# A split-precision projection stream on Trainium2: GpSimd's low halves of two k-tiles in one instruction

## The reference

```python
def hybrid_layer(x, norm_g, w_in, w_out, ...):
    h = rms_norm(x, norm_g)
    p = jnp.einsum('btd,dp->btp', h, w_in)          # (512, 2048) x (2048, 7192)
    (aq, ak, av, alr, az, bq, bk, bv, bz, cq, ck, cv, cz, dqkv, dbeta, da, dz) = jnp.split(p, offs, axis=-1)
    ya = gla_mixer(aq, ak, av, alr, ...) * jax.nn.silu(az)
    yb = swa_mixer(bq, bk, bv, ...) * jax.nn.silu(bz)
    yc = diff_mixer(cq, ck, cv, ...) * jax.nn.silu(cz)
    yd = gdn_mixer(dqkv, dbeta, da, ...) * jax.nn.silu(dz)
    y = jnp.concatenate([ya, yb, yc, yd], axis=-1)
    return x + jnp.einsum('btm,md->btd', y, w_out)  # (512, 2048) x (2048, 2048)
```

## Time and profile before

| | us |
|---|---|
| median of 3 runs | 1945.56 |
| lowest, highest | 1944.40, 1947.06 |
| the profiled execution | 1945.65 |
| its span, first to last instruction | 1943.7 |
| TensorE busy (matmuls) | 1919.0 |
| GpSimd busy | 919.0 |
| of it the low halves, 576 instructions | 753.5 |
| of it the issue of 288 fetches | 163.7 |

### The profile page before, as it was taken

One profiled execution on the slowest core, in us unless ns is written; L12 is line 12 of the kernel. 1 busy time (PEld: TensorE's weight loads), 2 busy tenths in 40 slices (PEclk: granted clock), 3 DMA queues, 4 the chain that ended last, 5 costly groups with the idle time before them and its releaser, 6 DMA issues.

```text
span 1943.7 us, 25935 instructions
## 1 busy us (share of the span) xinstructions
PE 1919.0 (99%) x10824; PEld 1554.6 (80%) x10824; DVE 682.7 (35%) x1234; ACT 495.5 (25%) x998; POOL 919.0 (47%) x876
## 2 busy tenths in 40 slices
PE   6999999999999999999999999999999999999999
PEld 5888788778888888777888887788788888887787
DVE  2656233223111343543324561332231113435442
ACT  4110222022222343322221011222132224433230
POOL 3555443444555543444554554434445554444454
PEclk9999999999999999999999999999999999999999
DMA  8566454545555556555775665444455555564556
GB/s 277 158 192 194 132 148 133 149 134 152 172 166 171 163 152 217 152 152 168 220 224 151 194 174 152 140 136 137 141 162 167 168 167 172 152 228 139 153 172 197
DMA packets 92180, 326.94 MB, mean 168 GB/s; under 512 B 10174, under 2 KB 10912, under 8 KB 91040
## 3 DMA queue, kind: packets, MB, share of 16 engines
q0 software_dynamic: 41472, 151.01, 27.4%
q1 hardware_dynamic: 44288, 155.75, 26.4%
q10 hardware_dynamic: 6304, 18.52, 2.5%
HBM read 316.86 MB, written 8.39 MB: 167 GB/s over the span
## 4 chain that ended last, share of the span: by engine, by line
PE 96%; ACT 2%; DMA 1%; DVE 1%; issue 0%; SPq 0%
PE acc L492 81%; PE mix L769 1%; PE mix L788 1%; DMA slots<-in_x 1%; PE mix L582 1%; PE mix L569 1%; PE mix L861 1%; PE mix L573 1%; PE mix L831 1%; PE mix L747 1%; PE mix L816 1%; PE mix L717 1%; PE mix L599 1%; PE mix L552 1%; PE mix L544 1%; PE mix L779 0%
## 5 line engine op out<-in xcount | busy, mean ns | idle before, releaser
L453 POOL TENSOR_TENSOR w_lo<-w_raw,w_hi 128x512 fp32r<-128x512 f32 x576 | 753.5, 1308 | 692.7 <-DMA w_hi<-in_wstream 525.9
L492 PE MATMUL acc<-w_hi,actT_hi 128*128 128x512 f32 x1920 | 781.7, 407 | 2.9 <-ACT slots L943 2.9
L492 PE MATMUL acc<-w_hi,actT_lo 128*128 128x512 f32 x1920 | 750.8, 391 | 0.0
L492 PE MATMUL acc<-w_lo,actT_hi 128*128 128x512 f32 x1920 | 749.4, 390 | 0.0
L492 PEld LDWEIGHTS acc<-w_hi,actT_hi 128*128 128x128 f32 x1920 | 361.0, 188 | 92.1 <-issue 22.1
L492 PEld LDWEIGHTS acc<-w_hi,actT_lo 128*128 128x128 f32 x1920 | 360.4, 188 | 78.3
L492 PEld LDWEIGHTS acc<-w_lo,actT_hi 128*128 128x128 f32 x1920 | 361.6, 188 | 65.0
L435 POOL DMA_DIRECT2D w_hi<-in_wstream x288 | 163.7, 568 | 322.6 <-PE acc L492 317.7
L492 PE MATMUL acc<-actT_hi,w_hi 128*128 128x512 f32 x384 | 152.1, 396 | 0.0
L492 PE MATMUL acc<-actT_hi,w_lo 128*128 128x512 f32 x384 | 149.8, 390 | 0.0
L492 PE MATMUL acc<-actT_lo,w_hi 128*128 128x512 f32 x384 | 149.6, 390 | 0.0
(11 more groups left out here) (247 smaller groups left out, 1699.6 us busy)
## 6 DMA issues: line engine op xcount, KB each, us to landing
w_hi<-in_wstream POOLq DMA_DIRECT2D x288, 512.0 KB, 3.9
w_raw<-in_wstream SPq DMA_DIRECT2D x288, 512.0 KB, 4.5
out_x<-slots ACTq DMA_DIRECT2D x7, 1024.0 KB, 8.2
slots<-in_x SPq DMA_DIRECT2D x4, 1024.0 KB, 15.5
slots<-in_x ACTq DMA_DIRECT2D x1, 4096.0 KB, 15.2
slots<-out_x ACTq DMA_DIRECT2D x1, 4096.0 KB, 15.7
out_x<-slots ACTq DMA_DIRECT2D x4, 256.0 KB, 2.2
cf_sb<-in_cf ACTq DMA_DIRECT2D x1, 933.0 KB, 11.3
```

The source lines that it names most:

```text
L453: pool.tensor_tensor(w_lo[:, n % RING], w_raw[:, g % RAW, k], w_hi[:, g % HI, k].bitcast(F32), ALU.subtract).then_inc(w_ready, 1)
L492: last = nc.tensor.matmul(acc[b][:, :], lhsT, rhs, start=(k == 0 and i == 0), stop=(k == kts - 1 and i == 2))
```

## The change

The two instructions of a pair become one over 1024 columns. It waits for the value of `kt_done` that the second of the two waited for (2g + 2), adds two to `w_ready`, and the fetch of w_hi for pair g + 1 is issued behind it. Nothing else differs: buffers, the other queues and the arithmetic are the same. The two k-tiles' buffers of `w_lo` lie next to each other (0 and 1, or 2 and 3).

```diff
                     pool.wait_ge(raw_in[g % RAW], g // RAW * 16 + 16)
                     pool.wait_ge(hi_in[g % HI], g // HI * 16 + 16)
-                    for k in range(2):
-                        n = 2 * g + k
-
-                        pool.wait_ge(kt_done, n + 1)
-                        pool.tensor_tensor(w_lo[:, n % RING], w_raw[:, g % RAW, k], w_hi[:, g % HI, k].bitcast(F32),
-                                           ALU.subtract).then_inc(w_ready, 1)
-                        if k == 0 and g + 1 < DEPTH * PAIRS:
-                            high_halves(g + 1)
+                    pe_done = 2 * g + 2
+                    pool.wait_ge(kt_done, pe_done)
+                    pool.tensor_tensor(w_lo[:, 2 * g % RING:2 * g % RING + 2], w_raw[:, g % RAW],
+                                       w_hi[:, g % HI].bitcast(F32), ALU.subtract).then_inc(w_ready, 2)
+                    if g + 1 < DEPTH * PAIRS:
+                        high_halves(g + 1)
```

## The result

The changed kernel takes 2271.65 us in the median of 4 runs (2263.41 to 2274.64), the kernel before 1944.98 us. The ratio is 1.167, with an interval of 1.164 to 1.170: slower by 327 us. The forecast was 2122 us with a range up to 2240, so the direction and the loop that sets the time held; the price of one member of that loop, the landing of w_hi's fetch, did not.

What follows compares the result with a forecast made beforehand. TensorE's matmuls bound the kernel, GpSimd's weight loop just ahead; lengthened to 7.07 us a pair, it costs 81 us in layer 0, 90 in layer 1 and 5 at the start: 176 us on 1945.65, so 2122 us, range 2030 to 2240.

Steps and rivals of the forecast that it cites:

- GpSimd's loop of operation, issue and landing: Weight supply on GpSimd: 5.47 us a pair before, 7.07 after; pairs with less TensorE work than that wait.
- The long operation: GpSimd's low halves: one 1024-column operation takes 2.40 us, between 2.29 and 2.59, replacing two of 1.295 us.
- The move as the cause: GpSimd's queue: the w_hi fetch, issued behind a 1.29 us operation before, now stands behind 2.40 us, lengthening each turn.
- Both fetches released within 0.1 us: GpSimd's w_hi and SyncE's raw fetch: one operation's end releases both; before, the raw issue came 1.92 us later.
- the landing of 4.5 us: w_hi's fetch, issue to landing, overlapping the raw fetch: 4.5 us likeliest, ends 3.9 and 5.1, against 3.9 before.
- the prediction's own table: Stretches of pairs with TensorE's time per pair; those under the loop's 7.07 us lose the difference: 81 and 90 us by layer.
- the 5 us of the start: First turns of the kernel: fetches take 5.3 to 7.0 us there, so 5 us were added to the sum.
- a sign of an error: TensorE's waits in the 7.48 us stretches, landings at 3.9 or over 5, or granted clock under 1.00 would show it wrong.
- the one of full hindrance: Rival on the two weight fetches: they hinder each other fully, loop 7.6 to 7.86 us, 2227 to 2300 us; chance 0.10.
- Cheap overlap: Rival on the two weight fetches: little hindrance, short operation, loop 6.39 to 6.6 us, 2005 to 2032 us; chance 0.09.
- not slower: Rival on w_hi's fetch: it gets quicker or its issue doesn't wait, time 1946 us; chance 0.03, of which 0.01 faster.
- The clock: Rival on TensorE: pauses every pair drop its clock to 1.2 GHz, some 700 us more, 2830 us; chance 0.02.

Runs made afterwards that it cites:

- the fetch first: Changed kernel with the next w_hi fetch issued ahead of the 1024-column operation instead of behind it: 1954.45 us, ratio 1.005.
- the move alone: Kernel before, two 512-column operations kept, with the next w_hi fetch issued behind the second instead of the first: 2294.10 us, ratio 1.178.
- the head start: Changed kernel with a small memset behind each w_hi issue; the raw fetch waits for it, issued 0.8 us after w_hi's: 2045.49 us, ratio 1.051.

## Why the prediction was wrong in its size

- *TensorE sets the end, GpSimd's loop of operation, issue and landing has no slack beside the short pairs.* Right. The chain that ended last consists of that loop now, and the landing and the operation as measured, pair by pair, followed through the loop and TensorE's own work of before, give 2253 us for the last k-tile's end, measured 2258.
- *The long operation, 2.40 us.* Right: 2384 ns in the mean, 2373 in the median.
- *The move as the cause, not the long operation.* Right: with the fetch first the loss is 10 us, with the move alone 349.
- *Both fetches released within 0.1 us.* Right, 0.08 us.
- **The step that failed: the landing of 4.5 us, with an end of 5.1.** It measured 5.0 in the median and 5.2 in the mean of the 280 fetches after the start. The working added 1.2 us ahead of the first byte, 2.65 us for both fetches at 395 GB/s, the rate of many queues at once, and 0.6 us behind the last byte: 4.45. The middle term is the one that was mis-sized; the two others came out shorter. In the changed kernel the first raw packet starts 1.04 us after w_hi's issue, from there to w_hi's last packet it is 3.59 us, and 0.37 us later the fetch lands. The two don't fill the engines together, they go one behind the other, at about 290 GB/s over both, with 236 GB/s while the raw fetch moves alone. Who goes first decides the rest: had it been w_hi's, its landing would be near 4.0, as with the head start. The raw fetch, issued 0.08 us later, gets its first packet out at 1.04 us, where w_hi's, undisturbed, needs 1.28. That quarter of a microsecond puts the raw fetch ahead. No row of before showed it: there the raw fetch starts beside w_hi's, 0.93 us after the end of its issue in place of 0.64. And the mean belongs in the sum, not the middle: each late fetch is lost for good in a loop without slack. Followed pair by pair, a landing of 5.0 throughout would end the last k-tile at about 2201 us, the mean of 5.19 at 2253.
- *Smaller misses.* The hop from landing to operation is 0.23 us now, where I had 0.11. And the landing of 5.1, with the operation at its likeliest 2.40, makes a loop of 7.67 us and by the prediction's own table 2251 us, over the end of the range at 2240. The rivals' times at 6.6, 7.6 and 7.86 us leave out the 5 us of the start, and the 0.7 us from the last bytes to the next operation are 0.93 by the rows that they were read from.
- *The price per stretch.* With 2.38 - 0.05 + 5.2 + 0.23 = 7.76 us in place of 7.07, the prediction's own table gives 158 + 168 us. Measured are 318. Layer 0 by stretch, forecast and measured: the start 11 and 11.7; the 19 short pairs 29.2 and 37.0; the 32 of 7.48 us 0 and 9.7; the 32 of 6.23 us 26.9 and 50.4; the 8 of 6.76 us 2.5 and 7.1; the 14 of 7.45 us 0 and 11.4; the 18 of 6.60 us 8.5 and 15.7; the last 8 pairs 7.7 and 17.8. The largest single miss, 23.5 us, is the 32 pairs of 6.23 us. Waits in the stretches of 7.48 us were named as a sign of an error, and they came.
- *The rival that came true* is the one of full hindrance, at 0.10: its loop of 7.6 to 7.86 us and 2227 to 2300 us hold the measured 7.8 and 2272. What was said for it, that a transfer can stand behind another one, is what happened; what was said against it, 2.65 us of work for both, is the term that failed.
- *Cheap overlap and not slower* fell with the 5.0 us. *The clock* did fall, in part, and cost next to nothing; see below.

## What to carry to other kernels

Where one engine's operation, the issue of the next fetch and that fetch's landing form a loop, add its members up before moving one behind another: the share of busy time (47% here) hides it. Look also at what else the same semaphore releases: the two transfers that start at one moment here don't share by halves, and 0.8 us of head start for the one that is waited for was worth 225 us. If two operations are merged, keep the issue ahead of them; that made the difference between 10 us and 327 us.

## What the hardware showed that I had not expected

A fetch issued by GpSimd, 128 rows of 4 KB, has its first packet 1.28 us after the issue, one issued by SyncE 0.64 us after the end of its own (0.97 after the start). When both are issued within 0.1 us, 128 rows of 4 KB each, SyncE's is served first and GpSimd's starts at 2.7 us. 64 rows of 4 KB beside it are worse than 128 rows (landing 5.5 against 5.0 us), which I can't explain.

The granted clock. It stayed full in the earlier trace rows; in the changed kernel it falls to half in 28 short stretches between 28 and 2241 us, 3.4 us long, two of them 6.8. One of them, with the pause of TensorE ahead of it (timeline, then stretches with the clock as third from the right):

```profile
697.41 0.50 PE L490 MATMUL acc<-w_hi,actT_hi 128*128 128x512 f32 x1 [2.09 <-POOL w_lo L451]
...
697.80:701.20 3.40, 3.40 (x10) 2.63 (x9) 0.00 (x0) 0.00 (x0) 0.08 (x1) 0.50 0.84 277
701.20:705.00 3.80, 3.75 (x17) 2.80 (x16) 0.00 (x0) 2.25 (x4) 2.65 (x2) 0.99 0.08 28
```

Ten matmuls start in 3.4 us at 1.2 GHz, seventeen in the 3.8 us behind it at 2.4. Every fall stands at a pause of 1.8 to 5.8 us, and the pause ahead of that was often 1 to 2 us too. But of the 42 pauses of 1.8 us or more 16 had no fall beside them. The k-tiles touched by a fall grow by about 49 us together. That cost the kernel almost nothing, because the same k-tiles wait for the loop anyway: with or without their growth, the sum over all pairs ends within 1 us of 2253. The Trainium skill (TensorE: Matmul & The Clock Gate, Part 1) has the gate open with activity and close without it, and the trace agrees that pauses of this length can close it, though not each does; the 1.7 us of the earlier trace rows didn't.
